# Last gates, late gate and new states in another order, and a residual that comes back in eight pieces

## What is computed

```python
x = x + 0.5 * _swiglu(_rmsnorm(x, norm_ffn1_g), ffn1_w_up, ffn1_w_down)
u = _rmsnorm(x, norm_mix_g);  P = u @ w_in    # lru_x | lru_gate | z | xBC | dt | gate logits
y_lru = gelu(lru_gate) * rglru(conv(lru_x))
y     = rmsnorm_by_group(ssd_scan(silu(conv(xBC)), dt, A, h0) * silu(z))
m = sigmoid(gA) * (y_lru @ w_br_lru) + sigmoid(gB) * (y @ w_br_ssd)
x = x + m @ w_out
x = x + 0.5 * _swiglu(_rmsnorm(x, norm_ffn2_g), ffn2_w_up, ffn2_w_down)
return rmsnorm(x, norm_final_g), conv tails, h of both branches
```

## Time and profile before

| | |
|---|---|
| three runs, median (lowest, highest) | 1964.55 us (1963.19, 1965.55) |
| the profiled execution | 1961.23 us |
| its span, first to last instruction | 1959.6 us |
| mean granted TensorE clock | 0.987 |
| PE busy | 1897.9 us, 97% |
| DVE, ACT, POOL busy | 1059.9, 738.1, 113.7 us |
| DMA moved | 175.61 MB, mean 90 GB/s |

### The profile page before, as it was taken

How to read it: one execution, slowest core, us unless ns; L and a number is a source line. 1 busy time by engine, 2 the same in 40 slices (tenths; PEclk the granted TensorE clock), 3 DMA queues, 4 the chain that set the end, 5 groups by cost and what they waited for, 6 DMA issues and landing times.

```text
span 1959.6 us, 31929 instructions
## 1 busy us (share of the span) xinstructions
PE 1897.9 (97%) x12877; PEld 1844.7 (94%) x12877; DVE 1059.9 (54%) x1339; ACT 738.1 (38%) x1157; POOL 113.7 (6%) x219
## 2 busy tenths in 40 slices
PE   8999999999799999999999999999799999999998
PEld 7999999999699999989989989998799999999998
DVE  6442443345688664766666676665645433442444
ACT  5221332123477744454445535533333221221222
POOL 2000000000012110001101001000000000000000
PEclk9999999999899999999999999999999999999999
DMA  4222222222322242243243234234622222222222
GB/s 142 75 66 74 75 75 75 75 70 81 102 69 66 73 131 79 85 138 95 73 121 112 71 92 131 80 92 127 228 74 76 75 75 75 75 75 75 76 62 78
DMA packets 269794, 175.61 MB, mean 90 GB/s; under 512 B 6726, under 2 KB 259834, under 8 KB 269405
## 3 DMA queue, kind: packets, MB, share of 16 engines
q1 hardware_dynamic: 239840, 129.52, 22.9%
q0 software_dynamic: 7072, 26.34, 4.4%
q10 hardware_dynamic: 22800, 18.62, 3.0%
HBM read 151.99 MB, written 22.45 MB: 89 GB/s over the span
## 4 chain that ended last, share of the span: by engine, by line
PE 48%; issue 4%; DVE 3%; ACT 2%; DMA 0%; POOL 0%; DVEq 0%; ACTq 0%; POOLq 0%
PE pu L630 43%; PE pn L837 1%; PE pn L827 1%; PE pn L855 1%; PE pn L878 1%; PE pn L887 1%; ACT w_hi L973 0%; PE pn L859 0%; DVE xf L1371 0%; PE pn L815 0%; PE pn L939 0%; PE pn L647 0%; DVE bc L1371 0%; PE pu L939 0%; DMA merged<-gate_spill 0%
## 5 line engine op out<-in xcount | busy, mean ns | idle before, releaser
L630 PE MATMUL pu<-act_hi,w_hi 128*128 128x320 f32 x2336 | 544.6, 315 | 20.0 <-ACT act_hi L1000 7.4
L1377 DVE TENSOR_TENSOR w_lo<-w_raw,w_hi 128x1024 fp32r<-128x1024 f32 x240 | 294.7, 1228 | 489.8 <-ACT w_hi L973 487.4
L630 PE MATMUL pu<-act_lo,w_hi 128*128 128x320 f32 x2336 | 535.5, 311 | 2.3 <-DVE act_lo L1418 2.1
L630 PE MATMUL pu<-act_hi,w_lo 128*128 128x320 f32 x2336 | 535.6, 311 | 0.0
L973 ACT ACTIVATE w_hi<-w_raw 128x1024 fp32r<-128x1024 f32 x240 | 253.5, 1056 | 509.4 <-PE pu L630 503.4
L630 PEld LDWEIGHTS pu<-act_hi,w_hi 128*128 128x128 f32 x2336 | 393.4, 189 | 38.9 <-issue 31.3
L630 PEld LDWEIGHTS pu<-act_lo,w_hi 128*128 128x128 f32 x2336 | 393.3, 189 | 3.9 <-DVE act_lo L1418 3.5
L630 PEld LDWEIGHTS pu<-act_hi,w_lo 128*128 128x128 f32 x2336 | 393.5, 189 | 0.0
L630 PE MATMUL pu<-h_hi,w_hi 128*128 128x320 f32 x1056 | 241.2, 310 | 0.7 <-DVE ff_g L1435 0.7
L630 PE MATMUL pu<-h_lo,w_hi 128*128 128x320 f32 x1056 | 241.2, 309 | 0.0
L630 PE MATMUL pu<-h_hi,w_lo 128*128 128x320 f32 x1056 | 240.9, 309 | 0.0
(11 more groups left out here) (323 smaller groups left out, 1945.3 us busy)
## 6 DMA issues: line engine op xcount, KB each, us to landing
w_raw<-in_ffn_w_up_dram SPq DMA_DIRECT2D x87, 512.0 KB, 3.8
w_raw<-in_w_in_dram SPq DMA_DIRECT2D x73, 512.0 KB, 3.9
w_raw<-in_ffn_w_down_dram SPq DMA_DIRECT2D x32, 512.0 KB, 3.9
w_raw<-in_w_br_ssd_dram SPq DMA_DIRECT2D x16, 512.0 KB, 3.5
w_raw<-in_ffn_w_down_dram SPq DMA_DIRECT2D x16, 384.0 KB, 3.4
gate_spill<-gbuf ACTq DMA_DIRECT2D x18, 320.0 KB, 2.2
es<-e_spill POOLq DMA_DIRECT2D x40, 128.0 KB, 3.0
merged<-gate_spill POOLq DMA_DIRECT2D x8, 640.0 KB, 5.5
```

What stands on the lines that cost most here:

```text
L630: ins = pe.matmul(dst[:, h, :], w[:, side, c, :], a[:, k, h * HALF:(h + 1) * HALF], start=(at == 0), stop=(at == n - 1))
L1377: dve.tensor_tensor(w_lo[:, side, :, :], w_raw[:, side, :, :], w_hi[:, side, :, :].bitcast(F32), ALU.subtract).then_inc(s["w_lo_done"], 1)
```

## The change

- `LAST_UNITS` becomes `gl` 6, `gl` 7, `gs` 7. ACT fetches gate 7's branch block before the third `yn_hi` step, does `gl` 7 behind the third and `gs` 7 behind the fourth; DVE does `gl` 7 behind the third scaling instead of the second unit behind the second.
- On PE the calls between the tiles of `middle` move from behind tiles 0, 2, 3, 4, 6 to behind 0, 1, 2, 4, 5, and those of `late` from behind 1 and 4 to behind 0 and 2.
- ACT does the late unit before the square of the streams' part. DVE does `new_state(2)` between reading the late output and the cut behind it.
- POOL's DMA of the whole residual goes. SP fetches it in eight pieces of 320 KB, one behind each output unit's weight load; piece k (from 2 on) waits until output k-2 is free. The loop of SP is unrolled. DVE waits for piece k before `resid` k. SP waits for the last `yn_lo` before the first output unit's load.

```diff
@@ -61,7 +61,7 @@
                [[("z", g, 1)], [("z", g, 2)], [("z", g, 3)], [("xb", g + 1, 5)]],
                [[("xb", g + 1, 4)], [("br", g - 1, 1)], [("br", g - 1, 2)], [("br", g - 1, 3)]],
                ("gs", 2 * g - 2), ("gs", 2 * g - 1), ("gl", g + 1))
-LAST_UNITS = (("gl", 6), ("gs", 7), ("gl", 7))
+LAST_UNITS = (("gl", 6), ("gl", 7), ("gs", 7))
 GATE_AFTER = 2
 
 
@@ -144,7 +144,7 @@
 hist_in ext_in conv tail_in wg_in gates_mm lru_v lru_a htail_in spill e_out es_in0 es_in1 yl_hi_done yl_lo_done
 dt_v dt_a dt_p gtr xb_th xb_out z_th m_built ht_zero ssd_p ssd_a ssd_v bseq
 h0_in0 h0_in1 hs_step old_mm old_cp hs_out0 hs_out1 hp_mm hp_cp hp_out yz yn_hi_done yn_lo_done br_s gl_th gl_out0 gl_out1 gl_in gs_th gs_out
-ma_in0 ma_in1 mg_b mg_v mh_done ml_done reload tail_mm tail_cp tails_out gfin fin_a fin_v y_a y_v y_dma""".split()
+ma_in0 ma_in1 mg_b mg_v mh_done ml_done reload0 reload1 tail_mm tail_cp tails_out gfin fin_a fin_v y_a y_v y_dma""".split()
 
 
 def feature_tile(buf, i):
@@ -413,9 +413,12 @@
             load_fill(LAST_UNITS)
             for r in range(4):
                 load_branch(GROUPS - 1, r)
-            with sp.Fori(0, KT // 2) as i:
-                for k in range(2):
-                    load(k, U_OUT, 2, i, cols(w_out[0], i * 256 + k * P))
+            sp.wait_ge(s["yn_lo_done"], GROUPS * PAIRS)
+            for k in range(KT):
+                load(k % 2, U_OUT, 2, k // 2, cols(w_out[0], k * P))
+                if k >= 2:
+                    sp.wait_ge(s["out_free"], O_OUT + k - 1)
+                sp.dma_start(x_res[:, k, :], x_spill[:, k * TOK:(k + 1) * TOK]).then_inc(s[f"reload{k % 2}"], 16)
             load_ffn(*FFNS[1], False)
 
             for t in range(NT):
@@ -593,7 +596,6 @@
                 pool.wait_ge(s[f"gl_out{m}"], KT * 8)
             for m in range(2):
                 load_merge(m)
-            pool.dma_start(x_res[:, :, :].rearrange("p k t -> p (k t)"), x_spill).then_inc(s["reload"], 16)
             for m in range(2, KT):
                 pool.wait_ge(s["ml_done"], m - 1)
                 load_merge(m)
@@ -905,10 +907,10 @@
                 inner(NT - 1)
                 pe.wait_ge(s["bseq"], g + 1)
                 new_state(0)
-                fill([middle], {0: lambda: old_state(0, 1), 2: lambda: from_state(0, 0), 3: lambda: old_state(1, 0),
-                                4: lambda: from_state(0, 1), 6: lambda: old_state(1, 1)})
+                fill([middle], {0: lambda: old_state(0, 1), 1: lambda: from_state(0, 0), 2: lambda: old_state(1, 0),
+                                4: lambda: from_state(0, 1), 5: lambda: old_state(1, 1)})
                 new_state(1)
-                fill([late], {1: lambda: from_state(1, 0), 4: lambda: from_state(1, 1).then_inc(s["ssd_p"], 1)})
+                fill([late], {0: lambda: from_state(1, 0), 2: lambda: from_state(1, 1).then_inc(s["ssd_p"], 1)})
                 new_state(2)
                 new_state(3)
 
@@ -1303,10 +1305,10 @@
                 states_out(0)
                 if late[0] == "gl":
                     fetch_branch(late[1])
+                fill([late])
                 act.wait_ge(s["yz"], g * SQG + SQG)
                 square_tile(SQ_GRP + g * SQG + PAIRS, 0, xf[:, 0:PAIRS, SEQ:TOK],
                             squares[:, 0, 0:PAIRS * P].rearrange("p (q c) -> p q c", q=PAIRS))
-                fill([late])
                 states_out(1)
                 if g < GROUPS - 1:
                     build_m(g + 1, 0)
@@ -1319,11 +1321,11 @@
             fill(LAST_UNITS[:1])
             for q in range(PAIRS):
                 if q == 2:
-                    fill(LAST_UNITS[1:2])
+                    fetch_branch(LAST_UNITS[1][1])
                 act.wait_ge(s["xn_done"], KT + q + 1)
                 act.activation(yn_hi[:, q, :], squares[:, q % 2, :], ACT.Copy).then_inc(s["yn_hi_done"], 1)
-            fetch_branch(LAST_UNITS[2][1])
-            fill(LAST_UNITS[2:])
+                if q >= 2:
+                    fill(LAST_UNITS[q - 1:q])
 
             def merged_split(m):
 
@@ -1645,7 +1647,7 @@
             def cut_behind(name):
                 cut_weights(U_AT[name] + 2, 0, 0)
 
-            def lru_gate(m):
+            def lru_gate(m, ahead=None):
 
                 ready_mix(("gl", m))
                 dve.wait_ge(s["gl_th"], m + 1)
@@ -1654,9 +1656,11 @@
                 else:
                     dve.wait_ge(s["gl_in"], 16 * (m - GATE_AFTER + 1))
                     stt(halves(gbuf[:, :]), out(O_AT["gl", m]), 1.0, halves(gbuf[:, :]), ALU.add, ALU.mult).then_inc(s["out_free"], 1)
+                    if ahead:
+                        ahead()
                 cut_behind(("gl", m))
 
-            def lru_branch(m):
+            def lru_branch(m, ahead=None):
 
                 ready_mix(("bl", m))
                 if m >= GATE_AFTER:
@@ -1858,8 +1864,7 @@
                 sv(NT - 1, SV_Y_LAST)
                 ys = xf[:, 0:PAIRS, SEQ:TOK]
                 dve.tensor_tensor(ys, ys, sz[:, :, SEQ:TOK], ALU.mult).then_inc(s["yz"], 1)
-                fill([late])
-                new_state(2)
+                (lru_gate if late[0] == "gl" else lru_branch)(late[1], lambda: new_state(2))
                 new_state(3)
                 dve.wait_ge(s["sq_done"], SQ_GRP + g * SQG + SQG)
                 sampled_sum = rvar[:, SEQ:TOK]
@@ -1893,7 +1898,7 @@
                     dve.wait_ge(s["yn_lo_done"], (GROUPS - 1) * PAIRS + q - 1)
                 stt(squares[:, q % 2, :], xf[:, q, :], v(V_SNG + (GROUPS - 1) * PAIRS + q), rstd[:, :],
                     ALU.mult, ALU.mult).then_inc(s["xn_done"], 1)
-                if q == 1:
+                if q == 2:
                     fill(LAST_UNITS[1:2])
             for q in (2, 3):
                 split_last(q)
@@ -1917,12 +1922,12 @@
                     dve.wait_ge(s["mg_b"], k + 1)
                     dve.tensor_tensor(part, part, gate, ALU.add).then_inc(s["mg_v"], 1)
             merged_lo(KT - 1)
-            dve.wait_ge(s["reload"], 16)
             dve.wait_ge(s["ml_done"], KT)
             clear_sum(1 + GROUPS)
             with dve.Fori(0, KT // 2) as i:
                 for k in range(2):
                     take(U_OUT + k, O_OUT + k, 2, 2, i)
+                    dve.wait_ge(s[f"reload{k}"], i * 16 + 16)
 
                     stt(halves(feature_tile(resid, i * 2 + k)), out(O_OUT + k), 0.5,
                         halves(feature_tile(x_res, i * 2 + k)), ALU.mult, ALU.add).then_inc(s["out_free"], 1)
```

## The result

The changed kernel takes **1944.89 us** (median of 5 runs, 1944.65 to 1947.25), against 1963.93 (5 runs, 1962.10 to 1965.55) for the kernel before: 19.0 us less, a ratio of 0.9906 (0.9892 to 0.9921). The forecast was 1943. Its profiled execution is the slowest of the five: 1947.25 us, span 1945.6. Lines of the changed kernel are shifted: L630 is L632, L897 is L899, L973 is L975, L984 is L986, L1175 is L1177, L1371 is L1373, L1377 is L1379, L1708 is L1714, L1785 is L1791, L1839 is L1845, L1860 is L1866, L1887 is L1892, L1916 is L1921, L589 is L592; the new pieces are L421.

What follows compares the result with a forecast made beforehand. PE was busy 97% of the span, so only its idle gaps and its slow-clock stretches could shorten the kernel without less arithmetic. Gains 12.2 + 7.0 + 4.2 - 2.0 = 21.4 off 1964.55 gave 1943 us, range 1937 to 1953.

Steps and rivals of the forecast that it cites:

- Part 1, group ends: Ends of the four groups: PE starts the last new state and next unit earlier, 3.2 + 3 x 3.0 = 12.2 us gained.
- The costs entered at nothing (masks, square later): Group ends: ACT's masks and `yn_hi` before the next weight cuts, and its later square, were to delay PE by 0.
- Part 2, clock: Units behind groups 1 to 3: with the clock staying at 1.00 they take what they took after group 0, 7.0 us gained.
- the short gap there, 0.39: Group 0: 0.39 us idle within the small matmuls, no clock fall; the change was to leave 0.75 instead of 1.9.
- Part 3, last gates and merge: From the last gates to the end of the merge: 4.2 us gained of its own.
- 2.9 and 0.7: Merge: 2.9 us gained by the third load taking 5.3 without the reload, 0.7 by POOL no longer issuing it first.
- Now the fetch lies under the third scaling: Last gates: the fetch of gate 7's block, for which DVE had waited, was to be covered by the third scaling.
- the order at +0.6 less 0.5: Last gates: the new order gains 0.6 us at the following branch block and costs 0.5 at POOL's first merge load.
- I take the clock to hold: Merge: PE's 6.1 us wait splits into several of under 3, and the clock was assumed not to fall.
- the merge gains nothing: Rival, chance 0.10: the third merge load is late for another reason, such as stores and weights beside it; 1946 us.
- Part 4, the pieces: Output units: weight loads held and queued behind residual pieces come 0.85 us late per unit, over six units; 2.0 us lost.
- the 3.6 that the forecast hides: Output units: PE needs the freed output 3.6 us after `resid` 0, so 3.6 of the 5.1 lateness is hidden.

Runs made afterwards that it cites:

- e5: The changed kernel with only PE's calls between the tiles of `middle` and `late` put back as before: 1946.98 us, ratio 0.9921 to the kernel before.
- e6: The changed kernel with only ACT's square of the streams' part put back ahead of the late unit: 1945.38 us, ratio 0.9914 to the kernel before.
- e8: The changed kernel with PE's tiles, ACT's order and `new_state(2)` at the group ends all put back as before: 1964.64 us, ratio 1.0009 to the kernel before.
- e7: The changed kernel with only `new_state(2)` put back behind DVE's cut of the late unit's weights: 1955.67 us, ratio 0.9955 to the kernel before.
- e1: The changed kernel with the whole residual on POOL again, after merge loads 0 and 1, no pieces: 1946.67 us, ratio 0.9914 to the kernel before.
- e4: The changed kernel with the whole residual fetched by one POOL DMA behind the last merge load, no pieces: 1941.46 us, ratio 0.9890 to the kernel before.
- e3: The changed kernel with piece k waiting until piece k-2 has landed, not until output k-2 is free: 1943.38 us, ratio 0.9899 to the kernel before.

## Why the prediction came out right, by its steps

**Part 1, group ends: right, 12.45 for 12.2.** ACT's and DVE's timelines in group 1, against the earlier trace rows:

```profile
1005.52 0.77 ACT L1177 ACTIVATE pu<-pu,vec 128x640 f32<-128x640 f32 x1 [10.67 <-PE pu L632]
...
1007.69 0.63 ACT L986 ACTIVATE squares<-xf 128x512 f32<-128x512 f32 x1 [0.43 <-DVE gbuf L1373]
```

```profile
1003.71 0.69 DVE L1866 TENSOR_TENSOR xf<-xf,sz 128x512 f32<-128x512 f32 x1
1006.38 0.82 DVE L1373 SCALAR_TENSOR_TENSOR gbuf<-pu,gbuf 128x640 f32<-128x640 f32 x1 [1.98 <-ACT pu L1177]
1007.12 1.21 DVE L1845 TENSOR_TENSOR h_b<-h_b,pu 128x1024 f32<-128x1024 f32 x1
1008.25 1.22 DVE L1379 TENSOR_TENSOR w_lo<-w_raw,w_hi 128x1024 fp32r<-128x1024 f32 x1
```

The tanh runs when the unit ends, the gate at once, `new_state(2)` ahead of the cut. The steps hold one by one: this trace is 1.6 us ahead of the one before where the group end begins, so the 1002.7 and 1006.0 that were forecast for DVE's L1785 and the end of L1860 are 1001.1 and 1004.4 here, and its timeline has 1001.09 and 1004.40. What the sum did not see is that its steps cover for each other: with ACT's order in place, the tiles have no part in the gap of 1.9 (e5), and the other way round (e6). Undone one by one the three parts are worth 2.8 (tiles), 0 (ACT's order) and 9.6 (`new_state(2)`: 5.1 of gaps and 4.5 of clock), and 19.0 all together (12.4 and 6.6 by the columns). Of the 6.6 that are left over, 3.6 are the three gaps before the last new state (3 x 1.2), which tiles and ACT's order close jointly; most of the rest is clock, and that differs between executions. The costs entered at nothing (masks, square later) show in no wait.

**Part 2, clock: the number right, 6.96 for 7.0; the reason not shown.** "The clock fell around the gap before the last new state; after group 0 it did not fall", and the forecast took the short gap there, 0.39, for the reason. It left out the gap behind group 0's new states, which is the longest of all, and at which the clock held (PE's timeline; then window rows, with the granted clock third from the right):

```profile
849.26 0.53 PE L630 MATMUL pu<-act_hi,w_hi 128*128 128x320 f32 x2 [2.23 <-DVE h_b L1839]
```

```profile
847.00:849.00 2.00, 0.04 (x2) 0.00 (x0) 2.00 (x2) 0.00 (x0) 0.00 (x0) 1.00 0.61 209
...
1010.00:1012.00 2.00, 1.37 (x4) 0.30 (x4) 1.92 (x3) 0.63 (x1) 0.12 (x1) 0.82 0.57 210
1012.00:1014.00 2.00, 0.96 (x5) 0.87 (x4) 2.00 (x2) 0.00 (x0) 0.00 (x0) 0.50 0.50 129
```

In group 1 it fell right behind the gap of 1.91, before the one of 1.04 behind the new states. With the gap of 1.9 it fell in six group ends of six (three here, three in e8). In e7, where that gap was 0.7, it fell all the same behind the 1.40 of groups 2 and 3 and once behind a wait of 0.52, and not behind the 1.40 of group 1 or the 1.58 of group 0. So neither the one gap nor the sum of the idle time decides by itself. With 0.7 and nothing behind it the clock held in groups 1 to 3 of all eleven kernels that have these ends. That the change gives the full 7.0 is shown, then; that it does so for the reason given is not, and what decides whether a wait brings a fall stays open.

**Part 3, last gates and merge: wrong, 0.96 for 4.2.** The third merge load did land as forecast, 5.1 for 5.3, and e1 puts the gain of taking the reload out of its way at 3.07, where 2.9 and 0.7 were entered (the load itself, 7.9 against 5.1, gives 2.8). Two other steps failed:
- "Now the fetch lies under the third scaling", with the order at +0.6 less 0.5. It does not: DVE is there 2.76 too early, and the first branch block starts 0.92 late. The row of the fetch, 3.0 us, was from a quieter moment; here it takes 4.3. Behind it, the first merge loads' 5.0 became 7.0, which the sum did not look at.
- "I take the clock to hold". The one 6.1 us wait became several under 3 as said, and the mean clock stayed at 0.92 (0.93 before). The shortfall, 3.2, is about what the rival "the merge gains nothing" takes off (2.9), but its reason, a third load late for something else, is not what happened.

**Part 4, the pieces: mechanism right, size 3.4 for 2.0.** SP in the changed kernel, and its issues of 1408 to 1412 us, against the earlier trace rows:

```profile
1408.83 0.34 SPq L421 DMA_DIRECT2D x_res<-x_spill  x1
1409.21 0.43 SPq L345 DMA_DIRECT2D w_raw<-in_w_out_dram  x1
```

```profile
w_raw<-in_w_out_dram SPq DMA_DIRECT2D x1, 512.0 KB, 4.4
x_res<-x_spill SPq DMA_DIRECT2D x1, 320.0 KB, 3.2
```

The load takes 4.4 behind a piece, 3.7 alone, and a unit is late by 7.93 - 7.04 = 0.89, where 0.85 was forecast (0.27 for a held load alone and 0.58 for the piece ahead; measured about 0.1 and 0.75). The Trainium skill (DMA: Bandwidth & Descriptors, Specifications) states a ceiling of 435 GB/s, by which the estimate was 0.65 per unit; the trace is nearer to the 0.85 by the rate of the earlier trace rows. One reading under this was wrong, though the sum does not hang on it: the load issued at 1426.94 in the kernel before is that of unit 4 and not 3, and its cut is at 1438.53; the loads had 7.9 us in hand, not 0.85, and the hold takes all of it. The mis-sized term is what the lateness adds up to: by the last cut, 1453.95, it is 48.20 - 6 x 7.04 = 6.0 and not 5.1, because the second FFN's first weight load, behind the last piece, is late by another 1.45. PE's own waits show 2.1 of it, the two below and one of 0.4 for `h_lo` at 1464.82:

```profile
1448.56 0.56 PE L632 MATMUL pu<-act_hi,w_hi 128*128 128x320 f32 x2 [0.47 <-DVE resid L1373]
...
1457.11 0.53 PE L632 MATMUL pu<-h_hi,w_hi 128*128 128x320 f32 x2 [1.24 <-DVE w_lo L1379]
```

PEld, whose weight loads stand ahead of the matmuls, waited longer at each of these places (0.74 us at the first, 1.48 at the second) and twice more where PE's view lists nothing. Its waits between 1433 and 1467 us have the whole (total, times, longest):

```profile
PEld pu L632 <- DVE w_lo L1379: 1.5, 1, 1.5
PEld pu L632 <- DVE resid L1373: 1.0, 2, 0.7
PEld pu L632 <- DVE h_lo L1373: 0.7, 1, 0.7
PEld pu L632 <- ACT h_hi L1355: 0.3, 1, 0.3
```

The first two are 2.4, which is the lateness of 6.0 less the 3.6 that the forecast hides; it had 1.5 there. The last two are 1.0 for `h_hi` and `h_lo` of the second FFN's first unit; it had 0.5. Together they are the 3.4.

So the forecast of 21.4 against 19.0 is two parts that held to 0.3 us and carry all of the time (e8: without them 1964.64), and two that were meant to bring 2.2 and, by the stretches, cost 2.5, by e8 about nothing. By the stretches the forecast is 4.4 too high; that the medians put it only 2 us off is partly luck, since they differ by 2 us from the stretches.

## What to carry to other kernels

When two engines take turns at the end of a stage, write out which operation frees the next matmul, put that one first on each engine, and cost the reorderings jointly: here either of two was enough for one gap, and the third, a state update put ahead of a weight cut, carried half the gain (9.6 of 19.0). A transfer that collides with others is better moved as a whole to a quiet moment (e4), or cut up with nothing held (e3), than cut up and held on a semaphore in a queue with weight loads behind it: the hold takes from these loads the whole lead that the queue had, here over 7 us, and the bytes are the smaller part. And take landing times for a moved DMA from a stretch as loaded as the one it is moved into.

## What was not expected of the hardware

- The same two waits around the last new state (0.72 and 1.40 us in e7) left the granted clock at 1.00 after group 1 and not after groups 2 and 3: 14.31 against 15.86 us for 96 matmuls, and 8.72 against 7.28 for 48. The runs of that kernel reach from 1951.29 to 1958.04. A longer wait, 2.23 us behind group 0's new states in the kernel before, left the clock at 1.00, and so did it in e8.
- Code that no experiment touches differs by up to 4.4 us between profiled executions (-0.86 to +3.58 against the kernel before), much of it slow stretches of the clock before the mixer and near the end of the program: from 558 to 562 us the mean granted clock is 0.57 in the changed kernel and 1.00 in the kernel before. Below about 2 us only stretches of the trace can be compared, not totals.
